# Denominator operations of the attention steps issued later, zero rows moved from the queries to the keys, and a later start of the first merge, in a two-layer encoder on eight cores

## The reference

```
h = rmsnorm(x); [qa ka va | qb kb vb | ga gb] = h @ w_in
branch A: 8 heads of 64; three windows, (128, step 1), (512, step 4), (2048, step 16);
          o_p, den_p per pattern from exp(q.k + bias); ya = sum_p(o_p * den_p) / sum_p(den_p)
branch B: 8 query heads on 2 key heads, window +-128, a sink term in the denominator -> yb
x += (sigmoid(ga) * (ya @ W_A) + sigmoid(gb) * (yb @ W_B)) @ W_out
x += (silu(n(x) @ W_gate) * (n(x) @ W_up)) @ W_down
x += sigmoid(n(x) @ W_pg) * (p[layer] @ W_pp)
```

## Time and profile before

| | us |
|---|---|
| median of 3 runs | 2429.97 (2425.39 to 2434.06) |
| the profiled execution | 2429.2 |
| its span, core 5 (cores: 2411.8 to 2427.6) | 2427.6 |
| PE busy | 2150.4 (89%) |
| DVE busy | 1266.5 (52%) |
| ACT busy | 906.5 (37%) |
| POOL busy | 181.2 (7%) |
| chain that ended last, by engine | PE 74%, ACT 8%, DVE 7%, issue 7%, DMA 3% |

### The profile page before, as it was taken

One profiled execution on the slowest core, in us unless ns is written; L12 is line 12 of the kernel. 1 busy time (PEld: TensorE's weight loads), 2 busy tenths in 40 slices (PEclk: granted clock), 3 DMA queues, 4 the chain that ended last, 5 costly groups with the idle time before them and its releaser, 6 DMA issues.

```text
span 2427.6 us, 33456 instructions; the slowest of 8 cores (2411.8 to 2427.6 us)
## 1 busy us (share of the span) xinstructions
PE 2150.4 (89%) x11264; PEld 1051.6 (43%) x11264; DVE 1266.5 (52%) x2107; ACT 906.5 (37%) x1569; POOL 181.2 (7%) x197
## 2 busy tenths in 40 slices
PE   4777767999999999999887777789998999999998
PEld 1554542434444444444345544334443444444444
DVE  5776767556451122126886777675664412211376
ACT  3566568444221101111445666785431211011123
POOL 3110000001000000100130100000000010000000
PEclk9988889999999999999998888999999999999999
DMA  9540314446545301531253413313554354025113
GB/s 227 90 53 18 50 37 80 52 54 106 86 53 74 46 7 18 74 53 27 82 101 71 47 24 53 83 22 53 71 103 77 46 74 53 1 36 74 18 27 139
DMA packets 233793, 149.23 MB, mean 61 GB/s; under 512 B 87515, under 2 KB 211579, under 8 KB 233595
## 3 DMA queue, kind: packets, MB, share of 16 engines
q0 software_dynamic: 152240, 85.01, 27.7%
q1 hardware_dynamic: 81388, 62.08, 8.7%
HBM read 211.07 MB, written 21.00 MB: 96 GB/s over the span
## 4 chain that ended last, share of the span: by engine, by line
PE 74%; ACT 8%; DVE 7%; issue 7%; DMA 3%; ACTq 0%; DVEq 0%; POOL 0%; SPq 0%; POOLq 0%
PE ps L116 60%; PE ps L113 14%; DVE X L113 3%; ACT YP L113 3%; ACT scr L113 2%; DVE hT L113 2%; DVE YP L113 2%; ACT G L113 2%; DMA ring<-w_in 1%; DMA ring<-w_out 1%; ACT sq L113 1%; DMA G<-vscr 0%; ACT L113 0%; DMA vscr<-X 0%; DVE G L113 0%
## 5 line engine op out<-in xcount | busy, mean ns | idle before, releaser
L116 PE MATMUL ps<-hT,ring 128*128 128x512 bf16 x4536 | 1140.0, 388 | 15.4 <-DVE hT L113 7.1
L116 PEld LDWEIGHTS ps<-hT,ring 128*128 128x128 bf16 x4536 | 448.2, 100 | 518.6 <-issue 47.7
L113 ACT ACTIVATE scr<-ps 128x512 f32<-128x512 f32 x496 | 285.3, 596 | 970.3 <-PE ps L113 935.0
L113 DVE TENSOR_TENSOR G<-ps,scr 128x512 bf16<-128x512 f32 x176 | 113.4, 686 | 478.8 <-PE ps L113 478.6
L113 ACT ACTIVATE YP<-ps 128x512 bf16<-128x512 f32 x504 | 290.1, 592 | 177.2 <-PE ps L113 169.2
L116 PE MATMUL ps<-G,YP 128*128 128x512 bf16 x1280 | 297.2, 379 | 0.0
L113 DVE TENSOR_TENSOR YP<-YP,Ebuf 128x512 bf16<-128x512 bf16 x504 | 208.3, 422 | 153.7 <-ACT YP L113 149.1
L113 PE MATMUL ps<-hT,ring 128*128 128x512 bf16 x648 | 221.2, 386 | 0.0
L113 DVE TENSOR_TENSOR X<-ps,X 128x512 f32<-128x512 f32 x192 | 130.3, 688 | 165.2 <-PE ps L113 164.5
L116 PEld LDWEIGHTS ps<-G,YP 128*128 128x128 bf16 x1280 | 125.2, 98 | 151.0
L116 PE MATMUL ps<-YP,G 128*128 128x128 bf16 (+2 forms) x864 | 136.1, 258 | 51.8 <-DVE X L113 26.8
(11 more groups left out here) (82 smaller groups left out, 1841.7 us busy)
## 6 DMA issues: line engine op xcount, KB each, us to landing
ring<-w_in POOLq DMA_DIRECT2D x42, 512.0 KB, 9.0
X<-x SPq DMA_DIRECT2D x16, 1024.0 KB, 14.3
YP<-w_ffn_down POOLq DMA_DIRECT2D x8, 1408.0 KB, 17.6
ring<-w_ffn_gate POOLq DMA_DIRECT2D x20, 512.0 KB, 6.0
ring<-w_ffn_up POOLq DMA_DIRECT2D x20, 512.0 KB, 8.1
ring<-w_out POOLq DMA_DIRECT2D x8, 1024.0 KB, 10.2
xscr<-X SPq DMA_DIRECT2D x8, 1024.0 KB, 4.2
X<-xscr SPq DMA_DIRECT2D x8, 1024.0 KB, 12.4
```

What stands on the lines that cost most here:

```text
L113: self.prog[eng].append(lambda e, c=call, s=s: getattr(e, c[0])(*c[1], **c[2]).then_inc(s, 1))
L116: self.prog[eng].append(lambda e, c=call: getattr(e, c[0])(*c[1], **c[2]))
```

## The change

- `late` holds due steps. A branch-A Ln may go 3 steps after its sum, the Exp 4, the multiplies 6; in branch B the four operations 2, 3, 4 and 6. Still at most one is issued per step, in order.
- Queries have one buffer per pair with both heads' rows; keys have one per head, with 64 zero rows. Buffer b of both, and two of the four value stages, lie in tile b of X. The clearing on POOL follows.
- `merge0` starts at step 53 of branch B in place of 50, after a flush of `late`, and its budget per step is its cost over 41 in place of 46.

The diff, cut to its core (the other lines follow from these names):

```diff
@@ -251,9 +251,9 @@
...
-qpad = [[Xb(0, (2 * b + u) * 4096, 4096, BF16) for u in range(2)] for b in range(2)]
-kbuf = [Xb(1, b * 5120, 5120, BF16) for b in range(2)]
-vst = [Xb(1, 10240 + i * 1024, 1024, BF16) for i in range(4)]
+qv_ = [Xb(b, 10240, 4096, BF16) for b in range(2)]
+kbuf = [[Xb(b, u * 5120, 5120, BF16) for u in range(2)] for b in range(2)]
+vst = [Xb(i // 2, 14336 + (i % 2) * 1024, 1024, BF16) for i in range(4)]
@@ -497,13 +496,10 @@
...
 def q_dst(buf, n):
-    out = []
-    for u, rows in ((0, U0), (1, U1)):
-        out.append((rows, qpad[buf][u][rows, n * 512:(n + 1) * 512].rearrange("p (r s) -> p r s", r=16), True, [], [("q", buf, u, n)]))
-    return out
+    return [(ALLP, qv_[buf][:, n * 512:(n + 1) * 512].rearrange("p (r s) -> p r s", r=16), True, [], [("q", buf, n)])]
...
 def k_dst(buf, n):
-    return [(ALLP, kbuf[buf][:, 256 + n * 512:256 + (n + 1) * 512], False, [], [("k", buf, n)])]
+    return [(rows, kbuf[buf][u][rows, 256 + n * 512:256 + (n + 1) * 512], False, [], [("k", buf, n)]) for u, rows in ((0, U0), (1, U1))]
@@ -617,10 +613,14 @@
...
 late = collections.deque()
+now = [0]
+
+def late_add(delay, fn):
+    late.append((now[0] + delay, fn))
 
 def late_flush():
     while late:
-        late.popleft()()
+        late.popleft()[1]()
@@ -646,8 +646,9 @@
...
-            if late:
-                late.popleft()()
+            now[0] = i
+            if late and late[0][0] <= i:
+                late.popleft()[1]()
             fill.run(st["fill"])
@@ -692,8 +692,8 @@
...
-                lhsT = ap(kk, 256 + r, [[16, 128]])
-                rhs = ap(qpad[buf][u], 32 * r, [[512, 4], [1, 32]])
+                lhsT = ap(kbuf[buf][u], 256 + r, [[16, 128]])
+                rhs = ap(qv_[buf], 32 * r, [[512, 4], [1, 32]])
@@ -771,10 +771,10 @@
...
-                late.append(lambda: S.op("act", lambda e: e.activation(out=Dn[di][dst, :], in_=acc[u][den, sl], func=AF.Ln),
+                late_add(3, lambda: S.op("act", lambda e: e.activation(out=Dn[di][dst, :], in_=acc[u][den, sl], func=AF.Ln),
...
                 if u == 1:
-                    late.append(lambda: S.op("act", lambda e: e.activation(out=Dn[di][:, :], in_=Dn[di][:, :], func=AF.Exp, scale=-1.0),
+                    late_add(4, lambda: S.op("act", lambda e: e.activation(out=Dn[di][:, :], in_=Dn[di][:, :], func=AF.Exp, scale=-1.0),
...
-                    late.append(fin)
+                    late_add(6, fin)
@@ -828,7 +828,8 @@
...
                     if b < 8:
-                        late.extend(fin(b, oi))
+                        for dl, f in zip((2, 3, 4, 6), fin(b, oi)):
+                            late_add(dl, f)
@@ -1039,16 +1040,13 @@
...
-    def clear_x0():
-        S.alias(K_X0, R_X(0))
-        for b in range(2):
-            S.op("pool", lambda e, b=b: e.memset(qpad[b][0][U1, :], 0.0), reads=["pser"], writes=[("q0", b, 0), "pser"])
-            S.op("pool", lambda e, b=b: e.memset(qpad[b][1][U0, :], 0.0), reads=["pser"], writes=[("q0", b, 1), "pser"])
-
-    def clear_x1():
-        S.alias(K_X1, R_X(1))
-        for b in range(2):
-            S.op("pool", lambda e, b=b: e.memset(kbuf[b].rearrange("p (a t) -> p a t", a=10)[:, 0:10:9, :], 0.0), reads=["pser"], writes=[("kp", b), "pser"])
+    def clear_x(n):
+        S.alias(K_X01[n], R_X(n))
+        for u, z in ((0, U1), (1, U0)):
+            S.op("pool", lambda e, u=u, z=z: e.memset(kbuf[n][u][z, :], 0.0), reads=["pser"], writes=[("kp", n), "pser"])
+            v = U0 if u == 0 else U1
+            S.op("pool", lambda e, u=u, v=v: e.memset(kbuf[n][u].rearrange("p (a t) -> p a t", a=10)[v, 0:10:9, :], 0.0),
+                 reads=["pser"], writes=[("kp", n), "pser"])
@@ -1141,14 +1139,14 @@
...
-    q_merge = sum(c_ for c_, _ in merge0) / 46.0
+    q_merge = sum(c_ for c_, _ in merge0) / 41.0
     look = 3
@@ -1165,11 +1163,12 @@
...
     bs = b_steps(l, fill_of, pre_of, batch_of)
-    first8 = [i for i, s_ in enumerate(bs)][2 * 2 + 7 * 6 + look + 1]
+    first8 = [i for i, s_ in enumerate(bs)][2 * 2 + 7 * 6 + look + 4]
 
     def start_merge(old=bs[first8].get("pre")):
         if old:
             old()
+        late_flush()
         fill.add(merge0)
     bs[first8]["pre"] = start_merge
```

More of the change, by code:

```diff
@@ L281, in build @@
         R_X = lambda n: [("x", c, n) for c in range(NCH)]
-        K_X0 = [("q", b, u, n) for b in range(2) for u in range(2) for n in range(NTC)] + [("q0", b, u) for b in range(2) for u in range(2)]
-        K_X1 = [("k", b, n) for b in range(2) for n in range(NTC)] + [("kp", b) for b in range(2)] + [("vst", i) for i in range(4)]
+        K_X01 = [[("q", b, n) for n in range(NTC)] + [("k", b, n) for n in range(NTC)] + [("kp", b), ("vst", 2 * b), ("vst", 2 * b + 1)] for b in range(2)]
         K_X2 = [("acc", u, Q) for u in range(2) for Q in range(4)] + [("ob", i) for i in range(8)]
@@ L677, in pair_steps @@
             buf = c % 2
-            kk = kbuf[buf]
             KALL = [("k", buf, n) for n in range(NTC)] + [("kp", buf)]
@@ L683, in q_rd @@
             def q_rd(u, ns):
-                return [("q", buf, u, n) for n in ns] + [("q0", buf, u)]
+                return [("q", buf, n) for n in ns]
             def vcol(u):
@@ L715, in pair_steps @@
                     g = {}
-                    qv = qpad[buf][u]
+                    qv = qv_[buf]
                     qo = 512 * Q
@@ L731, in k1 @@
                     def k1(j):
-                        return ap(kk, 256 + 128 * j - 64, [[1, 128]])
+                        return ap(kbuf[buf][u], 256 + 128 * j - 64, [[1, 128]])
                     def k1rd(j):
@@ L758, in pair_steps @@
                                 c0 = rr * 256 + hf * 128
-                                lhsT = ap(kk, r + 512 * j, [[4, 128]])
+                                lhsT = ap(kbuf[buf][u], r + 512 * j, [[4, 128]])
                                 ns = set([max(512 * j - 256, 0) // 512, min(512 * j + 255, T - 1) // 512])
@@ L1071, in build @@
                     if n == 0:
-                        clear_x0()
+                        clear_x(0)
                     if n == 1:
-                        clear_x1()
+                        clear_x(1)
                         S.alias(K_X2, R_X(2))
@@ L1143, in build @@
             for n in range(2):
-                S.alias(R_X(n), K_X0 if n == 0 else K_X1)
+                S.alias(R_X(n), K_X01[n])
                 load_x(src_x, n, skey(n))
```

## The result

The changed kernel takes 2341.05 us by the median of 4 runs, beside 2432.01 us of the kernel before: a ratio of 0.9633 [0.9604, 0.9662], some 89 us or 3.7% faster. A few executions of most kernels, one of these four on either side among them, were disturbed and are several per cent longer; the ratios leave them out, the medians include them, and where a ratio stays wide I read the profiled execution. The three others of the changed kernel took 2339.62, 2339.88 and 2342.22 us. The forecast was 2378 us, 51 us faster. It had the side right, but the measured time lies at the very edge of the range (2340 to 2413): the median is 1 us inside it, and two of these three times are just outside.

What follows compares the result with a forecast made beforehand. Branch A was taken as bound by waits from queue order, no engine full. From 2429.2 us, -40.5 - 6 + 2 - 3 + 2.6 - 1.5 - 4.6 = -51 us gave 2378 us; range 2340 to 2413 us.

Steps and rivals of the forecast that it cites:

- Part 1: Late operations in branch A, both layers: -40.5 us for waits, -6 for PE's clock, +2 for the end flush.
- the clock: Branch A: less idle on PE lifts its granted clock, 3 us per layer, -6 us.
- the flush: End of branch A: more late operations wait for the final flush, ahead of branch B's first operations, +2 us.
- Part 2: Zeros moved to the keys: 10.3 us less DVE work in two layers, a third on the path, -3 us.
- Part 3: First merge: late start +2.6 us, denser filler over the logarithm batch -1.5, shorter drain -4.6.
- the batch wait: Merge: PE's 4.90 us wait behind the logarithms of blocks 8 to 11, 0.7 us more covered per layer, -1.5 us.
- The 3.10 us of the drain: Merge's drain: PE's stop for a bank DVE empties late goes, counted once whole and once half, -4.6 us.
- (a): Branch A: the waits only move, DVE's queue paces the steps, a third of 40.5 us remains; 2410 us, chance 0.17.
- (b): Branch A: all of PE's 81 us for ACT goes and 18 us of clock returns; 2325 us, chance 0.08.
- (c): Branch A: no change, each released wait returns at the next bias multiply; 2426 us, chance 0.05.
- (d): Branch A: slower, finishing multiplies delay the second head's sum and its bank, PE waits there; 2442 us, chance 0.06.
- (e): Branch A: score matmuls without zero rows lower PE's clock from 0.86 to 0.74; 2411 us, chance 0.02.

Runs made afterwards that it cites:

- e1: The kernel before with only branch A's late operations delayed (3, 4 and 6 steps): 2339.29 us, ratio 0.9629.
- e8: The changed kernel without the flush at the end of branch A, its late operations carried into branch B: ratio 0.9615, the same as its base.
- e2: The kernel before with only the zero rows moved from queries to keys: 2425.84 us, ratio 0.9988.
- e4: The changed kernel with the merge's start and budget and branch B's delays as before: 2341.09 us, ratio 0.9630.
- e3: The kernel before with only the merge started three steps later and its budget over 41: 2430.32 us, ratio 1.0004.
- e7: The changed kernel with the merge's budget over 46 as before, late start kept: 2345.61 us, ratio 0.9651.
- e6: The kernel before with only branch A's finishing multiplies moved from +3 to +6, behind the next sum: 2419.92 us, ratio 0.9947.
- e11: The kernel before with branch A's logarithms and exponential late (3, 4 steps), multiplies at +8, just ahead of a sum: 2348.4 and 2347.0 us.

## Why the prediction was right, and where its sizes failed

**The bound and the place** held. Branch A was bound by waits, the wait was the logarithm's in ACT's queue, and it went as named: 55 to 9 us. The sizes were too small, and that the range holds the result by 1 us is luck.

**Part 1, the branch A terms** (-40.5 us for the waits, -6 for the clock, +2 for the flush, -44.5 in all): measured -90 (e1). These are the terms that were mis-sized. I set the two ends of the first right (nothing, and the whole 55 us a layer) and chose half of PE's 41 us, "since only what reaches PE delays the next scores". That reading was too small: the stretch shortened by ACT's own wait, one to one. PE's own account on core 4 shows where the two terms failed. Its waits for ACT fell by 57 us in the two layers (28.6 in layer 0), two thirds of what there was and not half: -57 for -40.5. Its busy time, with the same 1659 matmuls in layer 0, fell by 20.5 and 18.5 us at a clock of 0.95 and 0.93 for 0.89 and 0.87: -39 for -6. So the term that was furthest off is the clock's, which I put near its low end.

That the clock is what shrank PE's busy time follows from the windows: in layer 0, (1 - 0.89) x 271.8 = 29.9 us were lost to the lower level before and (1 - 0.95) x 223.8 = 11.2 us after. That is 18.7 us less, beside the 20.5 of busy time. No kernel moved the clock alone, so that it came back because PE's gaps went is argued. Little was given back to DVE: its share of branch A rose from 70 to 81% (182.12 of 223.80; I named 76%), and PE's waits for it grew by 2.4 us.

The flush at the end (+2): the four multiplies in a row are there as said; in e8, removing them was worth nothing that could be told.

**Part 2, the keys** (-3 us): 2.9 us faster alone (e2), and nothing that the times can tell once the delays are in (e4 beside e1). The number came out by luck: branch A of e2 is 6.7 us shorter in the two layers, two thirds of the 10.3 us and not one third, and 2.2 us of it were lost ahead of the first scores, a term that I had not counted. The durations were right. By shape, in the changed kernel:

```profile
L113 DVE SCALAR_TENSOR_TENSOR X<-ps,vd,scr 128x512 bf16<-128x512 f32 x64 | 58.4, 913 | 46.2 <-ACT scr L113 43.8 <-PE ps L113 2.0 <-issue 0.2
L113 DVE SCALAR_TENSOR_TENSOR X<-ps,vd,scr 64x512 bf16<-64x512 f32 x64 | 47.9, 748 | 22.8 <-ACT scr L113 19.1 <-DVE X L113 0.5
```

The first mixes 32 strided query multiplies with 32 plain ones: 913 ns is the middle of 1071 and 750. With the earlier trace rows the sum fell from 116.5 to 106.3 us, by 10.2.

**Part 3, the merge** (+2.6 - 1.5 - 4.6 = -3.5 us): 1.0004 [0.9994, 1.0013] alone (e3), about +1 us, between -1.5 and +3. The step that failed is the batch wait. I had 4.90 us shrink by 0.7 a layer through denser filler; it became 6.63. In the changed kernel, ACT loads a table at 443.05, works through 12 operations of the batch, and loads the next at 452.92; PE meanwhile stands before a merge unit and is released by the gate's operation (ACT scr) behind them:

```profile
443.05 1.28 ACT L113 ACT_TABLE_LOAD   x1
...
452.92 1.28 ACT L113 ACT_TABLE_LOAD   x1
...
454.95 1.44 PE L116 MATMUL ps<-hT,ring 128*128 128x512 bf16 x3 [6.63 <-ACT scr L113]
```

The filler itself needs ACT, and its place against the batch had moved. With the budget over 46 the wait is 5.5 us (e7), so the budget explains 1.1 us of the 1.7. The 3.10 us of the drain went in layer 0 as said, but in layer 1 4.0 us stand in its place, where I had counted half of the 3.10 as saved. No run measured the +2.6 us of the late start by itself.

**The rivals.** (a) falls: PE's waits for DVE grew by 2.4 us only. (b), 2325 us, is nearer than the forecast, 16 us from the result for 37, but its parts are off too: it took all of PE's 81 us for ACT and 18 us of clock, and 57 and 39 came. (c) and (d) fall with e1, e6 and e11. (e) falls: with full query rows (e2) the clock of branch A was 0.88, not lower, and the run was faster. By the rule of the Trainium skill (TensorE: Matmul & The Clock Gate, Part 1, the note on the peak-current limiter) fewer zeros would have cost time; the trace does not agree with it.

## What to carry to other kernels

When an engine's queue holds an operation that nobody needs soon behind one that is late, look at the wait of the engine that waits, in full, if that engine feeds the chain, and not only at the idle time that PE shows for it. Here PE's idle time for ACT fell by 28.6 us in a stretch that fell by 48.0, since part of the loss stood in PE's slower work. Issue the operation some steps later, when its input is ready, and put long operations just behind the urgent one on their engine, not just ahead of it. Filler did not cover a batch on an engine that the filler itself needed: look at what it waits for.

## What was not expected of the hardware

Branch A with its many small gaps on PE ran at a granted clock of 0.89 and 0.87, and at 0.95 and 0.93 once 28 us of gaps a layer were gone; PE's busy time for the same matmuls fell by 20.5 and 18.5 us. The gaps that went in layer 0 on core 4 were those between 1.4 and 2.8 us: 22 of them, 42.6 us in all, before, and 7 of 13.6 us after. So the matmul time that went with the gaps, 20.5 us, was some three quarters of the idle time that went (27.5 us). No run moved the gaps and the clock apart.
